# Ten stages of two model blocks in one program: the borders of the last four stages taken by halves of the tokens

## The chip, the cores and the metric

The program runs on one core of a Trainium2 chip. Its time is the device time of one launch in microseconds; the number given is the median of the runs shown. The engines are TensorE (PE), VectorE (DVE), ScalarE (ACT), GpSimd (POOL) and SyncE (SP), which here only issues the DMAs. They work at the same time, and only semaphores order them against each other.

## What is computed

x is an array of 512 tokens by 1024 numbers. Two blocks are applied to it, one after the other, all in float32:

```python
def swiglu_ffn(x, g, w_in, w_out):
    h = rms_norm(x, g)
    gate, up = jnp.split(h @ w_in, 2, axis=-1)
    return (jax.nn.silu(gate) * up) @ w_out

# first block, layers 0 and 1
x = x + 0.5 * swiglu_ffn(x, ffn1_norm[l], ...)
x = x + retention_dilated_mixer(...)  if l == 0 else x + stick_breaking_mixer(...)
x = x + 0.5 * swiglu_ffn(x, ffn2_norm[l], ...)
# then rms_norm(x, final_norm); second block, layers 0 and 1
def hybrid_layer(x, mod, norm1, norm2, ...):
    shift1, scale1, gate1, shift2, scale2, gate2 = jnp.split(mod[:, None, :], 6, axis=-1)
    h = rms_norm_2(x, norm1) * (1.0 + scale1) + shift1
    proj = h @ w_in                      # u, q, k and v, gates
    mix = jnp.concatenate([y_pool, y_nsa], axis=-1) @ w_out
    x = x + gate1 * mix
    h2 = rms_norm_2(x, norm2) * (1.0 + scale2) + shift2
    ff = jnp.square(jax.nn.relu(h2 @ w_ff1)) @ w_ff2
    return x + gate2 * ff
```

rms_norm divides each token by the root of the mean of its squares, so nothing that a stage does with a token can start before all 1024 numbers of that token are there. It needs no other token. Each of the second block's layers is a mixer (sparse attention y_nsa and a pooling y_pool) and a squared-relu feed-forward.

## The kernel before

There are ten stages: F1_0, HYB, F2_0, F1_1, STICK, F2_1 (first block), then NSA_0, REL_0, NSA_1, REL_1 (second block; NSA is a mixer, REL a feed-forward). The change is about the four borders F2_1 to NSA_0, NSA_0 to REL_0, REL_0 to NSA_1 and NSA_1 to REL_1.

**Layout.** x stands in SBUF as s_x, 128 partitions (features) by 8 tiles d by 512 tokens. A product is computed from split numbers: a float32 is a high part and a low part that PE multiplies at full rate, and one step k of a product is three matmuls of 512 columns (tokens): high input by high weight, low input by high weight, high input by low weight (`product`, L807). h is s_hh and s_hl, the middle activation s_a0h/s_a0l or s_a1h/s_a1l, the weights s_wh and s_wl.

**Weights** come in units of up to 1024 columns through a ring of four (RING): SP issues the DMA into s_raw, ACT copies s_raw to s_wh (L1355) and DVE subtracts to get s_wl (L1756). A ("load", u) in a plan is the place at which ACT and DVE convert unit u, three units ahead of PE (AHEAD). Each adds about 1 us to what stands behind it in ACT's and DVE's queues.

**Order.** Nothing is scheduled by a program. For each stage a function (`plan_ffn` L131, `plan_nsa` L345, `plan_rel` L440) writes one list of steps by hand, and every engine walks it and does its own part of each step, waiting on semaphores for the others. What an engine does is thus in the order of the list, and a step that waits holds all behind it on that engine.

**End of a stage.** Output tile d (one unit of weights, 8, 6 or, in the last part of NSA, 2 steps k) is a product into a PSUM bank; ("add") is DVE's scalar_tensor_tensor of 512 tokens from PSUM onto x (L1773); ("tile") is ACT's square of that tile and POOL's running sum over tiles 0 to 5 in s_ssum. For NSA_0 there is a second set of squares and sums with the gains of final_norm. The last tile's add and its squares are done in two halves of 256 tokens. The last part of NSA ("late", L423 to 437) has eight units of 256 columns.

**Head of a stage.** ("mean"): PE multiplies the squares of tiles 6 and 7 and s_ssum with ones (`norm_halves`, L1087: 12 records of 256 columns, 24 for NSA_0), ACT makes the roots from it (L1410), for NSA_0 after two small DVE steps (L2041). ("scale", d): DVE makes s_x times s_rstd (TENSOR_TENSOR, for NSA_0 scalar_tensor_tensor), then times and plus s_mod (TENSOR_SCALAR); ACT makes s_hh from the first of the two, DVE s_hl as the second less s_hh. ("first", four): PE runs the first four units together (`four`, L1297): for each k the high products of all four, the low-weight ones, the low-input ones, as soon as s_hh and s_hl of tile k are there.

The functions that the change touches:

Of the kernel before, what the change touches and what calls it, by code (L numbers as in the profile page):

```python
# [2840 lines left out]
```

## Time and profile before

| | |
|---|---|
| three runs | 3094.01, 3096.35, 3094.82 us; median 3094.82 |
| the profiled execution, first to last instruction | 3093.8 us |
| mean granted clock of PE in it | 0.997 of full speed |
| busy: PE, DVE, ACT, POOL | 3056.1, 1673.5, 1109.1, 680.3 us |
| matmul records of PE | 14530 |

The span is the profiled execution's own time from its first to its last instruction. The medians are of other executions, and lie within 1.0 us of that span. In a timeline "[3.66 <-ACT s_hh L76]" says that the engine was idle for 3.66 us before this row, and that ACT's write of s_hh ended the wait. A matmul's record is longer than the distance to the next one, since they are pipelined. All names of lines are those of small helpers (L70 is every matmul, L79 every tensor_tensor), so rows are told apart by the names of their tiles.

### The profile page before, as it was taken

Reading aid. Unit: us, or ns where it says so; the run is one execution under the profiler, and the core shown is the slowest. Engines: PE = TensorE matmul, PEld = TensorE weight load, DVE = VectorE, ACT = ScalarE, POOL = GpSimd, SP = SyncE. Lnnn points to the kernel's source line nnn. Section 1 sums busy time; section 2 is a strip of 40 time slices with the busy share of each in tenths; the row PEclk is TensorE's granted clock in tenths of the full one; section 3 lists DMA queues with packets and bytes.
Section 4 is the critical chain, followed back from the end, with each engine's and each line's share of the span. In section 5 each row is a group of like instructions: output and inputs, shape, how many; then the busy total and the mean of one; then the engine's idle time right before and its main releaser. Section 6 shows DMA issues by size and latency. Waiting matters only on the chain.

```text
span 3093.8 us, 36733 instructions
## 1 busy us (share of the span) xinstructions
PE 3056.1 (99%) x14530; PEld 2474.3 (80%) x14530; DVE 1673.5 (54%) x2491; ACT 1109.1 (36%) x1757; POOL 680.3 (22%) x525
## 2 busy tenths in 40 slices
PE   9999999999999999999999999999999999999999
PEld 7888887788888888887788888776788877778887
DVE  6454557554555445536864555677533356763332
ACT  4222344332223332244443222456422333643331
POOL 2101134111011110054211101356211123722110
PEclk9999999999999999999999999999999999999999
DMA  5343422243443334432043444301333331033332
GB/s 190 116 153 126 134 85 72 85 140 116 153 132 126 127 119 153 129 108 62 31 136 119 131 138 134 109 31 53 105 96 96 97 105 62 17 108 102 96 95 75
DMA packets 115802, 329.70 MB, mean 107 GB/s; under 512 B 13616, under 2 KB 19120, under 8 KB 115248
## 3 DMA queue, kind: packets, MB, share of 16 engines
q1 hardware_dynamic: 115632, 327.36, 33.1%
q8 instruction: 116, 1.90, 0.2%
q14 instruction: 54, 0.44, 0.0%
HBM read 325.21 MB, written 2.10 MB: 106 GB/s over the span
## 4 chain that ended last, share of the span: by engine, by line
PE 92%; DVE 4%; ACT 2%; POOL 1%; issue 1%; DMA 0%; DVEq 0%; SPq 0%; ACTq 0%; POOLq 0%
PE ps L70 90%; PE ps L73 1%; ACT s_tmp L76 1%; POOL s_tmp L87 1%; DVE s_tmp L79 1%; DVE s_wl L79 1%; DVE s_tmp L99 0%; ACT s_wh L76 0%; DVE s_small L93 0%; ACT s_hh L76 0%; DVE s_x L82 0%; DVE s_tmpr L79 0%; POOL s_tmp L79 0%; DVE s_hl L79 0%; ACT s_tmpr L76 0%
## 5 line engine op out<-in xcount | busy, mean ns | idle before, releaser
L76 ACT ACTIVATE s_wh<-s_raw 128x1024 fp32r<-128x1024 f32 (+3 forms) x560 | 541.8, 970 | 1109.3 <-PE ps L70 1107.2
L70 PE MATMUL ps<-s_hh,s_wh 128*128 128x512 f32 x2304 | 894.6, 393 | 18.8 <-ACT s_hh L76 11.9
L79 DVE TENSOR_TENSOR s_wl<-s_raw,s_wh 128x1024 fp32r<-128x1024 f32 (+3 forms) x529 | 607.8, 1150 | 532.6 <-ACT s_wh L76 532.3
L70 PE MATMUL ps<-s_hh,s_wl 128*128 128x512 f32 x2304 | 887.7, 390 | 0.2
L70 PE MATMUL ps<-s_hl,s_wh 128*128 128x512 f32 x2304 | 886.9, 390 | 0.3 <-DVE s_hl L79 0.3
L79 POOL TENSOR_TENSOR s_tmp<-s_tmp 128x512 f32<-128x512 f32 (+2 forms) x228 | 315.8, 1389 | 1616.5 <-ACT s_tmp L76 1453.3
L70 PEld LDWEIGHTS ps<-s_hh,s_wh 128*128 128x128 f32 x2304 | 433.3, 188 | 116.0 <-issue 17.1
L70 PEld LDWEIGHTS ps<-s_hh,s_wl 128*128 128x128 f32 x2304 | 433.6, 188 | 93.0 <-DVE s_wl L79 2.9
L70 PEld LDWEIGHTS ps<-s_hl,s_wh 128*128 128x128 f32 x2304 | 433.7, 188 | 92.2 <-issue 2.2
L70 PE MATMUL ps<-s_a0h,s_wh 128*128 128x512 f32 x960 | 377.3, 393 | 0.0
L70 PE MATMUL ps<-s_a0h,s_wl 128*128 128x512 f32 x960 | 373.8, 389 | 0.0
L70 PE MATMUL ps<-s_a0l,s_wh 128*128 128x512 f32 x960 | 373.7, 389 | 0.0
L70 PEld LDWEIGHTS ps<-s_a0h,s_wh 128*128 128x128 f32 x960 | 180.2, 188 | 38.6 <-issue 1.5
L70 PEld LDWEIGHTS ps<-s_a0h,s_wl 128*128 128x128 f32 x960 | 180.2, 188 | 37.8
L70 PEld LDWEIGHTS ps<-s_a0l,s_wh 128*128 128x128 f32 x960 | 180.3, 188 | 37.1 <-DVE s_a0l L79 0.3
L70 PE MATMUL ps<-s_a1h,s_wh 128*128 128x512 f32 x512 | 199.2, 389 | 0.0
L70 PE MATMUL ps<-s_a1l,s_wh 128*128 128x512 f32 x512 | 199.2, 389 | 0.0
L70 PE MATMUL ps<-s_a1h,s_wl 128*128 128x512 f32 x512 | 199.2, 389 | 0.0
L82 DVE SCALAR_TENSOR_TENSOR s_x<-ps,s_mod,s_x 128x512 f32<-128x512 f32 (+1 forms) x116 | 83.8, 729 | 196.5 <-PE ps L70 196.4
L79 DVE TENSOR_TENSOR s_a0l<-s_tmp,s_a0h 128x512 fp32r<-128x512 f32 x88 | 61.0, 693 | 170.9 <-ACT s_a0h L76 170.9
L82 DVE SCALAR_TENSOR_TENSOR s_x<-ps,s_x 128x512 f32<-128x512 f32 x129 | 88.2, 684 | 119.4 <-PE ps L70 119.4
L76 ACT ACTIVATE s_tmp<-ps 128x512 f32<-128x512 f32 (+6 forms) x258 | 132.9, 549 | 52.0 <-DVE s_tmp L79 20.2
(141 smaller groups left out, 2995.7 us busy)
## 6 DMA issues: line engine op xcount, KB each, us to landing
s_raw<-in_ff_dram SPq DMA_DIRECT2D x128, 512.0 KB, 3.6
s_tmp<-in_w_mod_dram SPq DMA_DIRECT2D x192, 256.0 KB, 3.5
s_raw<-in_f1i_dram SPq DMA_DIRECT2D x88, 512.0 KB, 3.6
s_raw<-in_f2i_dram SPq DMA_DIRECT2D x88, 512.0 KB, 3.6
s_raw<-in_f1o_dram SPq DMA_DIRECT2D x32, 512.0 KB, 3.5
s_raw<-in_f2o_dram SPq DMA_DIRECT2D x32, 512.0 KB, 3.4
s_raw<-in_hyb_dram SPq DMA_DIRECT2D x28, 512.0 KB, 3.5
s_raw<-in_nsa_dram SPq DMA_DIRECT2D x28, 512.0 KB, 3.6
```

The lines of the kernel that those rows point to most:

```text
L70: return self.eng.matmul(o, w, m, **kw) if self.eng is not None else Blank()
L73: return self.eng.transpose(*a) if self.eng is not None else Blank()
L76: return self.eng.activation(o, a, f, **kw) if self.eng is not None else Blank()
L79: return self.eng.tensor_tensor(o, a, b, f) if self.eng is not None else Blank()
L82: return self.eng.scalar_tensor_tensor(o, a, s, b, f, g) if self.eng is not None else Blank()
L87: return self.eng.tensor_scalar(o, a, s, t, f) if g is None else self.eng.tensor_scalar(o, a, s, t, f, g)
```

## The change

At the four borders the last output tiles are computed by halves of the tokens: of F2_1 tiles 5, 6 and 7, of REL_0 tiles 6 and 7, of both NSA the last part of all eight tiles. First comes tokens 0 to 255 of all these tiles, then 256 to 511 of all. Adds, squares and running sums of these tiles are by halves too.

The sum over tiles is one for each half (`sum_half` on PE; `norm_half` on ACT and DVE). That of tokens 0 to 255 stands before the end of the stage, among the last products ("next sum", "next mean"), and so do the first two tiles of the next stage's h for these tokens (`two_tiles`).

The next stage's first two units run by halves (`four`): for tokens 0 to 255 all eight high steps (four matmuls of 256 columns each), with the sum of tokens 256 to 511 behind the third, then all eight low-input steps (two matmuls each); then the same for 256 to 511. Units 3 and 4 run whole behind them, one after the other. The conversion of unit 3 stands between ACT's and DVE's scale steps and DVE's low steps of the second half, that of unit 4 behind the low steps (`head`).

s_hh and s_hl are made otherwise: DVE writes z = x times modulation times root (one scalar_tensor_tensor of 256 tokens), ACT adds the shift (s_hh), DVE makes s_hl from z, the shift and s_hh in one more. For that the gains of final_norm are multiplied into the modulation of NSA_0. The last part of NSA takes its weights as two units of 1024 columns, and uses four PSUM banks in turn (LATE_BANKS).

```diff
+HALVED = {F2_1: (5, 6, 7), NSA_0: tuple(range(KT)), REL_0: (6, 7), NSA_1: tuple(range(KT))}
+SUM_BANKS = {NSA_0: (6, 7), REL_0: (6, 7), NSA_1: (0, 1), REL_1: (6, 7)}
+LATE_BANKS = (4, 5, 2, 3)
+def two_tiles():
+    return [("next z", 0, 0), ("next h", 0, 0), ("next z", 1, 0), ("next h", 1, 0)]
+def head(four):
+    steps = []
+    for d in range(2, KT):
+        steps += [("z", d, 0), ("h", d, 0)]
+        if d == 4:
+            steps.append(("mean", 1))
+    steps += [("l", d, 0) for d in range(KT)]
+    for d in range(KT):
+        steps += [("z", d, 1), ("h", d, 1)]
+    return steps + [("load", four[2])] + [("l", d, 1) for d in range(KT)] + [("load", four[3])]
...
+                      ("half", 3, 6, u6, 1), ("add half", 3, 7, 0), ("tile half", 7, 0), ("next sum", 0),
+                      ("half", 3, 7, u7, 1), ("add half", 3, 6, 1), ("tile half", 6, 1), ("next mean", 0)] + two_tiles()
+                     + [("add half", 3, 7, 1), ("tile half", 7, 1)])
...
-    late = []
-    for d in range(KT):
-        u = stream.add(wo[d, :, 6 * 128:8 * 128], 256)
-        steps.append(("out", d, 6, 2, u))
...
+    late = [stream.add(wo[d:d + 4, :, 6 * 128:8 * 128].rearrange("d p c -> p d c"), 1024) for d in (0, 4)]
+    for n in range(2):
+        for d in range(KT):
+            steps.append(("half", 6, d, late[d // 4], n))
+            if d:
+                steps += [("add half", 6, d - 1, n), ("tile half", d - 1, n)]
+            if n == 0 and d == 1:
+                steps.append(("load", late[0] + AHEAD))
+            if n == 1 and d == 2:
+                steps.append(("next sum", 0))
+            if n == 1 and d == 3:
+                steps.append(("next mean", 0))
+            if n == 1 and d == 6:
+                steps += two_tiles()
+        steps += [("add half", 6, KT - 1, n), ("tile half", KT - 1, n)]
...
-            steps.extend([("mean",), ("scale", 0), ("load", four[3])] + [("scale", d) for d in range(1, KT)] + [("first", four)])
+            steps.extend(head(four) + [("first", four)])
...
+            def sum_half(s, n):
+                b, c = SUM_BANKS[s][n], HALVES[n]
...
+                for total, sig, slot, up, o, whole in sums:
+                    pe.wait_ge(*whole[sum_key(s, KT - 3, n)])
+                    pe.matmul(ps[:, b, o], ones[:, :], total[:, c], start=True, stop=False)
+                    for d in (KT - 2, KT - 1):
+                        pe.wait_ge(*sig[s, d, n])
+                        m = pe.matmul(ps[:, b, o], ones[:, :], S(slot(d))[:, c], start=False, stop=d == KT - 1)
+                    m.then_inc(*up.up((s, n)))
...
             def four(s, units_):
-                for k in range(KT - 2):
...
+                for n, c in enumerate(HALVES):
+                    for k in range(KT):
+                        cols = slice(k * 128, (k + 1) * 128)
+                        pe.wait_ge(*h_hi[h_key(s, k, n)])
+                        for u in units_[0:2]:
+                            pe.wait_ge(*w_hi[u])
+                            pe.matmul(ps[:, bank_of[u], c], wh[:, u % RING, cols], hh[:, k, c], start=k == 0, stop=False)
+                        for u in units_[0:2]:
+                            pe.wait_ge(*lo_of(u))
+                            pe.matmul(ps[:, bank_of[u], c], wl[:, u % RING, cols], hh[:, k, c], start=False, stop=False)
+                        if n == 0 and k == 2:
+                            sum_half(s, 1)
+                    for k in range(KT):
+                        cols = slice(k * 128, (k + 1) * 128)
+                        pe.wait_ge(*h_lo[h_key(s, k, n)])
+                        for u in units_[0:2]:
+                            m = pe.matmul(ps[:, bank_of[u], c], wh[:, u % RING, cols], hl[:, k, c], start=False, stop=k == KT - 1)
...
+            def scale(s, d, n):
...
+                if n:
+                    dve.wait_ge(*h_lo[s, d, "half"])
+                dve.scalar_tensor_tensor(scaled(d), x[:, d, c], mod[:, l, 3 * half + 1, d:d + 1], rstd[:, c], ALU.mult,
+                                         ALU.mult).then_inc(*h_scaled.up((s, d, n)))
...
+            def scale_lo(s, d, n):
...
+                dve.scalar_tensor_tensor(hl[:, d, c], scaled(d), mod[:, l, 3 * half, d:d + 1], f32(hh[:, d, c]),
+                                         ALU.add, ALU.subtract).then_inc(*h_lo.up(h_key(s, d, n)))
```

DVE's queue at the end of NSA_0, before: s_a0l is the last low part of the activation, s_wl a weight unit's low part, s_x the add of an output tile (signals: act_w_hi is ACT's conversion, pe_unit the end of a product).

```order
L79 TENSOR_TENSOR s_a0l<-ps,s_a0h 128x512 [waits act_a_hi]
L79 TENSOR_TENSOR s_wl<-s_raw,s_wh 128x256 [waits act_w_hi]
L82 SCALAR_TENSOR_TENSOR s_x<-ps,s_mod,s_x 128x512 [waits pe_unit]
L79 TENSOR_TENSOR s_wl<-s_raw,s_wh 128x256 [waits act_w_hi]
L82 SCALAR_TENSOR_TENSOR s_x<-ps,s_mod,s_x 128x512 [waits pe_unit]
L79 TENSOR_TENSOR s_wl<-s_raw,s_wh 128x256 [waits act_w_hi]
L82 SCALAR_TENSOR_TENSOR s_x<-ps,s_mod,s_x 128x512 [waits pe_unit]
L79 TENSOR_TENSOR s_wl<-s_raw,s_wh 128x256 [waits act_w_hi]
```

The same place now (pe_half is the end of a half product):

```order
L79 TENSOR_TENSOR s_a0l<-ps,s_a0h 128x512 [waits act_a_hi]
L79 TENSOR_TENSOR s_wl<-s_raw,s_wh 128x1024 [waits act_w_hi]
L82 SCALAR_TENSOR_TENSOR s_x<-ps,s_mod,s_x 128x512 [waits pe_unit]
L79 TENSOR_TENSOR s_wl<-s_raw,s_wh 128x1024 [waits act_w_hi]
L82 SCALAR_TENSOR_TENSOR s_x<-ps,s_mod,s_x 128x512 [waits pe_unit]
L82 SCALAR_TENSOR_TENSOR s_x<-ps,s_mod,s_x 128x256 [waits pe_half]
L79 TENSOR_TENSOR s_wl<-s_raw,s_wh 128x1024 [waits act_w_hi]
L82 SCALAR_TENSOR_TENSOR s_x<-ps,s_mod,s_x 128x256 [waits pe_half] x10
```

Three conversions of whole units stand where there was one of 256 columns for each add, and the last of them stands between the first and the second half add.

DVE's queue at the head of REL_0, before, from the first low step on (s_tmp is the scaled x):

```order
L79 TENSOR_TENSOR s_hl<-s_tmp,s_hh 128x512 [waits act_h_hi,dve_h_fine]
L79 TENSOR_TENSOR s_wl<-s_raw,s_wh 128x1024 [waits act_w_hi]
L79 TENSOR_TENSOR s_tmp<-s_x,s_rstd 128x512
L87 TENSOR_SCALAR s_tmp<-s_tmp,s_mod 128x512 [waits dve_h_scaled]
L79 TENSOR_TENSOR s_hl<-s_tmp,s_hh 128x512 [waits act_h_hi,dve_h_fine]
L79 TENSOR_TENSOR s_tmp<-s_x,s_rstd 128x512
L87 TENSOR_SCALAR s_tmp<-s_tmp,s_mod 128x512 [waits dve_h_scaled]
L79 TENSOR_TENSOR s_hl<-s_tmp,s_hh 128x512 [waits act_h_hi,dve_h_fine]
```

Now, from the scale steps of tokens 0 to 255 on:

```order
L82 SCALAR_TENSOR_TENSOR s_tmp<-s_x,s_mod,s_rstd 128x256 x6
L82 SCALAR_TENSOR_TENSOR s_hl<-s_tmp,s_mod,s_hh 128x256 [waits act_h_hi,dve_h_scaled] x8
L82 SCALAR_TENSOR_TENSOR s_tmp<-s_x,s_mod,s_rstd 128x256 [waits dve_h_lo,act_root2]
L82 SCALAR_TENSOR_TENSOR s_tmp<-s_x,s_mod,s_rstd 128x256 [waits dve_h_lo] x7
L79 TENSOR_TENSOR s_wl<-s_raw,s_wh 128x1024 [waits act_w_hi]
L82 SCALAR_TENSOR_TENSOR s_hl<-s_tmp,s_mod,s_hh 128x256 [waits act_h_hi,dve_h_scaled] x8
L79 TENSOR_TENSOR s_wl<-s_raw,s_wh 128x1024 [waits act_w_hi]
```

What went tile by tile now goes by phases of eight: scale steps, low steps, scale steps of the second half, the conversion of unit 3, low steps, the conversion of unit 4.

PE's queue at the head of REL_0, before:

```order
L70 MATMUL ps<-s_hh,s_wh 128x512 [waits act_h_hi,act_w_hi,dve_x_add]
L70 MATMUL ps<-s_hh,s_wh 128x512 [waits act_w_hi] x3
L70 MATMUL ps<-s_hh,s_wl 128x512 [waits dve_w_lo] x4
L70 MATMUL ps<-s_hl,s_wh 128x512 [waits dve_h_lo]
L70 MATMUL ps<-s_hl,s_wh 128x512 x3
L70 MATMUL ps<-s_hh,s_wh 128x512 [waits act_h_hi]
L70 MATMUL ps<-s_hh,s_wh 128x512 x3
L70 MATMUL ps<-s_hh,s_wl 128x512 x4
```

Now (s_ssum and s_tmp with s_ones are the sum of tokens 256 to 511):

```order
L70 MATMUL ps<-s_hh,s_wh 128x256 [waits act_h_hi]
L70 MATMUL ps<-s_hh,s_wh 128x256
L70 MATMUL ps<-s_hh,s_wl 128x256 x2
L70 MATMUL ps<-s_hh,s_wh 128x256 [waits act_h_hi]
L70 MATMUL ps<-s_hh,s_wh 128x256
L70 MATMUL ps<-s_hh,s_wl 128x256 x2
L70 MATMUL ps<-s_ssum,s_ones 128x256 [waits pool_ssum]
L70 MATMUL ps<-s_tmp,s_ones 128x256 [waits act_square] x2
L70 MATMUL ps<-s_hh,s_wh 128x256 [waits act_h_hi]
L70 MATMUL ps<-s_hh,s_wh 128x256
L70 MATMUL ps<-s_hh,s_wl 128x256 x2
```

Each step waits for one s_hh of 256 tokens and holds four matmuls of 256 columns where it held twelve of 512 with a wait for s_hl among them; the second sum stands between two steps.

## Rows read from the trace of the kernel before

**Rows 1.** The page's busy line: engine busy us (share of span) xinstructions.
```profile
PE 3056.1 (99%) x14530; PEld 2474.3 (80%) x14530; DVE 1673.5 (54%) x2491; ACT 1109.1 (36%) x1757; POOL 680.3 (22%) x525
```

**Rows 2.** PE's timeline: start, us, operation, count, idle before and releaser.
```profile
1955.64 2.04 PE L70 MATMUL ps<-s_hh,s_wh 128*128 128x512 f32 x4 [3.66 <-ACT s_hh L76]
...
2170.83 0.70 PE L70 MATMUL ps<-s_hh,s_wh 128*128 128x512 f32 x2 [2.99 <-ACT s_hh L76]
...
2525.18 1.25 PE L70 MATMUL ps<-s_hh,s_wh 128*128 128x512 f32 x4 [2.30 <-ACT s_hh L76]
```

**Rows 3.** Windows: us; PE, PEld, DVE, ACT, POOL busy (x); PEclk, DMA, GB/s.
```profile
1954.60:1961.40 6.80, 5.75 (x14) 4.53 (x15) 5.49 (x7) 2.56 (x4) 4.54 (x6) 0.50 0.94 329
...
2163.90:2174.20 10.30, 6.42 (x27) 4.38 (x25) 7.92 (x14) 7.95 (x14) 1.48 (x2) 1.00 0.54 177
```

**Rows 4.** PE's timeline: first matmul after the fourth unit, NSA_0 and NSA_1.
```profile
1980.22 0.39 PE L70 MATMUL ps<-s_wh,s_hh 128*128 128x512 f32 x1
...
2548.83 0.39 PE L70 MATMUL ps<-s_wh,s_hh 128*128 128x512 f32 x1
```

**Rows 5.** The chain of waits: start, us, operation, count.
```profile
1440.89 2.18 PE ps L73 x20
...
2174.11 345.75 PE ps L70 x1524
```

**Rows 6.** DVE's timeline at the adds named in the text.
```profile
1934.60 0.69 DVE L82 SCALAR_TENSOR_TENSOR s_x<-ps,s_x 128x512 f32<-128x512 f32 x1 [2.18 <-PE ps L70]
...
2153.29 0.75 DVE L82 SCALAR_TENSOR_TENSOR s_x<-ps,s_mod,s_x 128x512 f32<-128x512 f32 x1 [0.28 <-PE ps L70]
...
2509.01 0.75 DVE L82 SCALAR_TENSOR_TENSOR s_x<-ps,s_mod,s_x 128x512 f32<-128x512 f32 x1 [3.06 <-PE ps L70]
...
2519.89 0.88 DVE L82 SCALAR_TENSOR_TENSOR s_x<-ps,s_mod,s_x 128x256 f32<-128x256 f32 x2 [3.06 <-PE ps L70]
```

**Rows 7.** PE's timeline, the sum before NSA_0.
```profile
1946.64 2.32 PE L70 MATMUL ps<-s_tmp,s_ones 128*128 128x256 f32 x10
```

**Rows 8.** PE by form: count, busy us, mean ns, idle before and releaser.
```profile
L70 PE MATMUL ps<-s_tmpr 64*128 64x256 f32 x192 | 19.4, 306 | 2.7 <-DVE s_tmp L79 2.7
...
L70 PE MATMUL ps<-s_tmp,s_ones 128*128 128x256 f32 x40 | 10.7, 387 | 1.9 <-ACT s_tmp L76 1.9
```

**Rows 9.** PE's timeline, windows ending after two and three of one row's pairs.
```profile
2130.63 0.45 PE L70 MATMUL ps<-s_tmpr 64*128 64x256 f32 x4
...
2130.63 0.57 PE L70 MATMUL ps<-s_tmpr 64*128 64x256 f32 x6
```

**Rows 10.** ACT by form, 2164 to 2192, head of REL_0.
```profile
L76 ACT ACTIVATE s_wh<-s_raw 128x1024 fp32r<-128x1024 f32 x4 | 4.1, 1047 | 1.9 <-PE ps L70 1.9
...
L76 ACT ACTIVATE s_hh<-s_tmp,s_mod 128x256 fp32r<-128x256 f32 x2 | 1.1, 592 | 0.3 <-DVE s_tmp L79 0.3
...
L76 ACT ACTIVATE s_tmp<-ps,s_eps 128x256 f32<-128x256 f32 x2 | 0.9, 456 | 0.0
...
L76 ACT ACTIVATE s_rstd<-s_tmp 128x256 f32<-128x256 f32 x2 | 0.8, 416 | 0.1
...
L76 ACT ACTIVATE s_tmp<-s_x 128x256 f32<-128x256 f32 x2 | 0.7, 401 | 0.0
```

**Rows 11.** ACT's timeline, the first hh of REL_0.
```profile
2169.31 1.09 ACT L76 ACTIVATE s_hh<-s_tmp,s_mod 128x256 fp32r<-128x256 f32 x2 [0.26 <-DVE s_tmp L79]
```

**Rows 12.** DVE by form, 2168 to 2192, low parts of weight units.
```profile
L79 DVE TENSOR_TENSOR s_wl<-s_raw,s_wh 128x1024 fp32r<-128x1024 f32 x3 | 3.7, 1223 | 2.4 <-ACT s_wh L76 2.4
```

**Rows 13.** DVE by form, 1955 to 1976, with POOL at work and after.
```profile
L82 DVE SCALAR_TENSOR_TENSOR s_tmp<-s_x,s_gains,s_rstd 128x512 f32<-128x512 f32 x7 | 6.1, 870 | 0.0
...
L82 DVE SCALAR_TENSOR_TENSOR s_x<-s_x,s_gains,s_ssum 128x512 f32<-128x512 f32 x2 | 1.4, 747 | 0.0
```

**Rows 14.** DVE's timeline, the last a0l of NSA_0.
```profile
2150.98 0.69 DVE L79 TENSOR_TENSOR s_a0l<-ps,s_a0h 128x512 fp32r<-128x512 f32 x1 [3.20 <-ACT s_a0h L76]
```

**Rows 15.** POOL's timeline, two running-sum steps before REL_0.
```profile
2157.50 2.75 POOL L79 TENSOR_TENSOR s_ssum<-s_ssum,s_tmp 128x512 f32<-128x512 f32 x2 [0.73 <-ACT s_tmp L76]
```

More of the change, by code:

```diff
@@ L368, in plan_nsa @@
     four = [add_unit() for _ in range(4)]
-    steps += [("mean",), ("scale", 0), ("load", four[3])] + [("scale", d) for d in range(1, KT)] + [("x scale", d) for d in range(4)] + [("first", four)]
+    steps += head(four) + [("x scale", d) for d in range(4)] + [("first", four)]
     steps += [("load", four[3] + 1), ("copies", 0), ("load", four[3] + 2), ("copies", 1)] + [("x scale", d) for d in range(4, KT)] + [("u evac", 0), ("load", four[3] + 3)]
@@ L722, in last_add, with half_done @@
             p = {F1_0: 2, HYB: 1, F2_0: 2, F1_1: 2, STICK: 1, F2_1: 2, NSA_0: 6, REL_0: 3, NSA_1: 6}[s - 1]
-            return (s - 1, p, d) if half or finish_halves(s, d) == WHOLE else (s - 1, p, d, "half")
-        unit_at, bank_of = {}, {}
+            return (s - 1, p, d) if half or not halved(s, d) else (s - 1, p, d, "half")
+        unit_at, bank_of, half_bank = {}, {}, {}
+        def half_done(s, d, n):
+            u = unit_at[s, "half", d]
+            return unit[u] if n and (s not in (NSA_0, NSA_1) or d % 4 == 3) else half_up[s, d, n]
         def look_up():
@@ L905, in ffn @@
                         free[b] = [(x_add, (s, p, d))]
+                    elif kind == "half":
+                        half(s, *step[1:])
+                    elif kind == "next sum":
+                        sum_half(s + 1, 0)
                     elif kind == "modsum":
@@ L1113, in nsa @@
                     kind = step[0]
[L1114 to L1115 removed]
+                    if kind == "half":
+                        half(s, *step[1:])
+                    elif kind == "next sum":
+                        sum_half(s + 1, 0)
                     elif kind == "first":
@@ L1316, in rel @@
+                m.then_inc(*unit.up(u))
+                u, b = units_[3], bank_of[units_[3]]
+                claim(b)
+                product(b, u, h_of(s), range(KT), True, True).then_inc(*unit.up(u))
             def rel(s):
@@ L2418, in ffn @@
                         tile(s + 1, step[1])
+                    elif kind == "tile half":
+                        sum_tile(s + 1, step[1], step[2], HALVES[step[2]])
             def hyb(s):
@@ L2437, in hyb @@
                         tile(s + 1, step[1])
+                    elif kind == "tile half":
+                        sum_tile(s + 1, step[1], step[2], HALVES[step[2]])
             def stick(s):
@@ L2524, in nsa @@
                         tile(s + 1, step[1])
+                    elif kind == "tile half":
+                        sum_tile(s + 1, step[1], step[2], HALVES[step[2]])
             def rel(s):
@@ L2535, in rel @@
                         tile(s + 1, step[1])
+                    elif kind == "tile half":
+                        sum_tile(s + 1, step[1], step[2], HALVES[step[2]])
             for d in range(KT):
```

343 lines of the change are left out of this document (186 added, 157 removed).

## The prediction

> **What bounds the kernel now.** I read the page's busy line first [rows 1]: TensorE (PE) is busy 99% of the span, so the change can win only what PE loses at the four borders before and between the sparse stages, and it pays for all that it adds on PE. In the timeline of PE I looked at the first matmul behind each wait [rows 2]: it idles 3.66 us before the first unit of NSA_0, 2.99 before that of REL_0, 2.30 before that of NSA_1; REL_1 repeats REL_0. The windows show the granted clock [rows 3]: after the 3.66 us of idling it is 0.50, the 1.2 GHz level, for a stretch of 6.80 us; after the 2.99 us it stays at 1.00.
>
> What a border costs as a whole comes from its two ends. A matmul is shown 0.39 us long [rows 4] at a pace of 345.75/1524 = 0.227 [rows 5], so an add on VectorE (DVE), which waits for the shown end, starts 0.2 us after the slot of the product's last matmul. Border F2_1 to NSA_0: the product of tile 4 ends at 1934.60 - 0.2 = 1934.4 [rows 6], the fourth unit of NSA_0 at 1980.22 [rows 4]: 45.8 us. A record of the sums takes (2.32 - 0.387)/9 = 0.215 [rows 7, 8]. Work: 54 + 96 matmuls (34.1) and 24 records (5.2), 39.3; lost: 6.5, of it 2.8 to the clock: at half the clock each of the 14 matmuls that start in that stretch takes 0.2 more. NSA_0 to REL_0: the last early product ends at 2153.29 - 0.2 = 2153.1, the twelfth matmul of the head at 2174.11, 84 more take 19.1: 40.1 us for 48 + 96 matmuls and 12 records (35.3), lost 4.8. REL_0 to NSA_1: 2509.01 - 0.2 to 2548.83, 40.0 us for the same 35.3: lost 4.7. NSA_1 to REL_1 looks like the second. Lost at the four: 20.8 us. That is all there is to win.
>
> **The change part by part.** *Split products.* 54 matmuls of F2_1, 48 each of NSA_0, REL_0 and NSA_1, and 48 in each of four heads become two of 256 columns: 390 become 780. The sums keep their records. 512 columns at 2.4 GHz are 0.213 us, so 0.0135 of the 0.227 is a fixed part; 256 columns then cost 0.107 + 0.0135 = 0.120. Bounds: half of 0.227 is 0.1135 (nothing lost); above, of three pairs of 64-row matmuls with 256 columns two take 0.45 us and three 0.57 [rows 9]: the third adds 0.12, the second, with 0.306 for a lone one [rows 8], 0.144. That weights can be changed every 2.18/20 = 0.109 us is shown by the transposes [rows 5]. I take 0.120, the nearest row: 780 x 0.120 - 390 x 0.227 = 5.1 us (bounds 0 and 23.8).
>
> The trace has no full-height product of 256 columns. The Trainium skill ("TensorE: Matmul & The Clock Gate", Back-to-back issue gap) gives N/2.4 + 2.5 ns, 0.109 us at 256 and 0.216 at 512 columns. The trace disagrees at 512 with its 0.227. By the rule the split would cost 390 x 2.5 ns, 1.0 us (a rival below).
>
> *Prices off PE.* ACT: a half of hh 0.59, two in 1.09, so the next starts 0.50 later; a half square 0.40, the two root steps 0.46 and 0.42, a weight unit 1.05 [rows 10, 11]. DVE: low part of a weight unit 1.22 [rows 12]; a half scalar_tensor_tensor two in 0.88 [rows 6], which I read as 0.48 each with 0.40 between starts, an overlap of 0.08; an add of 512 columns 0.75, the next so 0.67 after its start. While POOL works beside it the 512 form takes 0.870 on average, else 0.747 [rows 13], and I put 0.50 for a half there. The new scale and low steps are such halves, 32 a border, 12.8 us at 0.40: just as much as what they hide behind, PE's first two units (96 x 0.120 = 11.5) and a sum (1.3), so they do not hide well.
>
> *End of NSA_0 (and of NSA_1).* A half product is 6 x 0.120 = 0.72 us. Its weights now come as two whole units, and three whole units (the second late one and REL_0's first two) are converted beside the first products. DVE: the last a0l ends at 2151.67 [rows 14]; ACT's unit, begun when its a0h is done, ends at 2151.9; low part to 2153.15, add 2153.8, low part 2154.95, add 2155.6, first half add 2156.05. ACT squares it (2156.45) and only then converts the fourth unit (2157.45); DVE's low part stands ahead of the second half add, which ends at 2159.1. PE has four banks for these products (LATE_BANKS); the sixth needs the bank of the second. It could start at 2153.1 + 4 x 0.72 + 0.1 + 0.72 = 2156.8: a new stall of 2.3 us, with 0.1 at the fifth. The sum of the first half waits for six steps of POOL, whole ones two in 2.75 us [rows 15], halves put at 0.7 to 0.9: 0 to 0.6, I take 0.3.
>
> *Head of the next stage.* PE's order: eight hh steps of 4 x 0.120 = 0.48 us each for tokens 0 to 255 with the second sum (1.3 us) behind the third, eight hl steps of 0.24, the same for 256 to 511, then two whole units (10.9 us). For REL_0:
> - hh 0 and 1 are made during the last products; 0.15 is lost.
> - hh 2 comes after the last half add (0.2 + 0.40), its scale step (0.47) and ACT (0.59): 1.7 us from the product's end against 0.96 of work: 0.6 to 0.75 lost.
> - On ACT the roots of the second half stand ahead of hh 5. After the sum: 0.2 + 0.46 + 0.42 + 0.59 with hand-overs is 1.7, against two steps of PE, 0.96: 0.7 lost.
> - DVE has the scale steps of the second half behind the last low step of the first. From there: eight scale steps 3.3, last hh 0.6, ACT's conversion of the third unit 1.05, its low part 1.22, and only then eight low steps 3.1: 9.3 us. PE's work from there is 2.0 + 3.84 + 1.92 = 7.8: 1.5 lost. The third unit is not needed before, but it stands in the queue ahead of the low steps, and everything behind them on PE waits.
>
> REL_0 so loses 2.4 + 0.3 + 0.15 + 0.6 + 0.7 + 1.5 = 5.7, against 4.8, and pays 96 x 0.0130 = 1.3 for its splits: +2.1; REL_1 the same. NSA_1 has no late weight stall (REL_0 halves only tiles 6 and 7): 0.75 + 0.7, and 2.5 behind the third unit, where POOL works beside it on the tables and half steps cost the 0.50 above: 4.0 against 4.7, splits 1.3: +0.5. NSA_0 has two more DVE steps and two more ACT steps in each root: 0.5 + 0.75 + 2.3, and 3.5 behind the third unit with POOL: 7.0 against 6.5, splits 1.4: +1.9. No single wait exceeds 2.4 us, so I count no fall of the clock there; the 2.8 us of before are in the 6.5.
>
> The larger late DMAs (512 KB in pieces of 1 KB) are issued over 5 us ahead; SP's tables move with the second sum; both cost nothing as long as that lead holds. Leading tiles in F2_1 and REL_0 feed sums in time.
>
> Sum: 2.1 + 2.1 + 0.5 + 1.9 = +6.6 us on a span of 3093.8. The runs' median, 3094.82, lies 1.0 above that span, so the time is 3094.8 + 6.6, about 3101.4 us. 6.2 us is 0.2%, about what a measurement of this kernel can tell from no change.
>
> **The rivals.**
> 1. *The borders really close* (faster). If a half step costs DVE and ACT half of a whole one (0.37 and 0.41) and the third unit's conversion fits between, the tail of the head vanishes (9 us of my 22.4) and the late stall shrinks from 2.4 to about 0.5 at two borders, the waits at the roots from 0.7 to 0.2 at four: 22.4 - 9 - 3.8 - 2 = 7.6 lost, 13.2 less than before, and 5.1 for the splits: -8, 3087 us. For it: the idle time before NSA_0's first unit is surely gone, hh 0 being made under the last product. Against: [rows 6, 10] show half steps at 60 to 70% of whole ones. It decides where the low steps of tokens 256 to 511 start before PE's hh steps end.
> 2. *A 256-column matmul is bound by its weight change* at 0.144 us [rows 8, 9]: 18.7 us more, of which about half fills waits counted above: +16, 3111 us. Against: the transposes' 0.109.
> 3. *The clock falls at the tails*, where PE is half busy for 3 us after a wait of 2: 2.8 us each by [rows 3], at two to four borders: 3107 to 3112. For it: the first line of [rows 3]; against: its second, with 2.99 us of idling and no fall.
> 4. *The fixed part is 2.5 ns*, the skill's gap above. As a mechanism of this kernel: 256 columns in half of 0.227, nothing lost by splitting (the low bound). PE then waits for DVE where it was late anyway, so only about half of the 5.1 comes back: 3099 us. The traced 0.227 speaks against a free split.
> 5. *The waits only change place* with no split cost showing: 3094 to 3096.
>
> **How the numbers follow.** Forecast 0.46 (3097 to 3107), rival 1 0.22, rival 2 0.10, rival 3 0.09, rival 4 0.08, rival 5 0.05. Of the forecast's 0.46, 0.23 lie above +6.2 us. Slower: 0.23 + 0.10 + 0.09 = 0.42; same: 0.23 + 0.08 + 0.05 = 0.36; faster: 0.22. The range 3087 to 3111 leaves out about half of rival 1 and of rival 2 and the end of rival 3.
>
> **What would show it.** In the profile after: 256-column products start 0.120 us apart (split); in NSA_0's end PE waits some 2 us once for DVE's s_x (late stall); in each head three waits on ACT's s_hh, at the third and sixth step, and one for DVE's s_hl or s_wl of about 1.5 us in REL and 2.5 to 3.5 in NSA; the granted clock stays 1.00 at 1954. I am wrong if the wait for s_hl is missing, or if the border from 2153.1 to the fourth unit's end is shorter than 40.1 us.

## The result and the profile after

| | before | changed |
|---|---|---|
| median of five runs | 3094.82 us (3093.3 to 3097.16) | 3110.21 us (3108.37 to 3110.98) |
| ratio, 95% interval | 1 | 1.0044 [1.0034, 1.0055] |
| profiled execution, span | 3093.8 us | 3108.6 us |

The changed kernel is 0.44% slower by the ratio (0.34 to 0.55%), 15.4 us by these medians and 14.8 by the spans. The forecast was 3101.4 us, with slower as the likeliest of three outcomes (0.42). The time lies 8.8 us above the forecast and 0.8 us inside the upper end of the range. The page's first lines, against [rows 1]:

```profile
span 3108.6 us, 37616 instructions
...
PE 3071.4 (99%) x14920; PEld 2503.2 (81%) x14920; DVE 1667.2 (54%) x2520; ACT 1112.6 (36%) x1792; POOL 679.8 (22%) x539
```

PE is busy 15.3 us longer, and its share is still 99%. This figure shows nothing of where: split matmuls overlap in the records, and matmuls at the lower clock count as busy. So I compared the starts of the same matmuls in the two timelines of PE, stage by stage. A border runs from the first matmul of the old stage's last output part to the first behind the new stage's fourth unit (for REL, to its first output product). The row "inside NSA_0" leaves out the stage's first 7.55 us, which are the same in all these kernels. The other kernels of the table are told of below.

| us | before | changed | x1 | x7 | x2 | x3 | x6 | x5 | x8 |
|---|---|---|---|---|---|---|---|---|---|
| F2_1 to NSA_0 | 66.65 | 69.09 | 69.09 | 70.62 | 66.35 | 68.48 | 66.34 | 63.49 | 62.94 |
| inside NSA_0 | 162.46 | 163.98 | 163.99 | 162.11 | 164.08 | 163.97 | 164.35 | 164.30 | 161.19 |
| NSA_0 to REL_0 | 108.34 | 112.46 | 110.09 | 109.19 | 110.80 | 112.22 | 107.34 | 106.60 | 106.49 |
| REL_0 to NSA_1 | 72.66 | 75.00 | 74.09 | 74.72 | 72.27 | 74.93 | 72.27 | 69.97 | 69.15 |
| inside NSA_1 | 171.93 | 171.48 | 171.30 | 171.83 | 169.86 | 171.78 | 172.04 | 169.85 | 171.78 |
| NSA_1 to REL_1 | 108.38 | 112.43 | 110.36 | 109.50 | 110.68 | 112.22 | 107.63 | 106.88 | 106.67 |

The insides of REL take 217.60 us in every kernel but x4. The changed kernel loses 2.4, 4.1, 2.3 and 4.1 us at the borders, 13.0 together where 6.6 was forecast, and 1.5 - 0.5 inside the two NSA stages; 0.9 more passes ahead of the first border, where nothing was changed. The ends of the new heads answer to [rows 4]:

```profile
1983.57 0.39 PE L70 MATMUL ps<-s_wh,s_hh 128*128 128x512 f32 x1
...
2560.16 0.39 PE L70 MATMUL ps<-s_wh,s_hh 128*128 128x512 f32 x1
```

PE's timeline shows the waits behind it (start, us, operation, count, idle before and releaser), against [rows 2]:

```profile
1959.21 0.53 PE L70 MATMUL ps<-s_hh,s_wh 128*128 128x256 f32 x1 [2.13 <-ACT s_hh L76]
...
2163.97 0.49 PE L70 MATMUL ps<-s_a0h,s_wh 128*128 128x256 f32 x1 [2.08 <-DVE s_x L82]
...
2177.08 0.39 PE L70 MATMUL ps<-s_hh,s_wh 128*128 128x256 f32 x1 [0.44 <-ACT s_hh L76]
...
2180.54 0.50 PE L70 MATMUL ps<-s_hh,s_wh 128*128 128x256 f32 x2 [0.47 <-ACT s_hh L76]
...
2188.27 3.27 PE L70 MATMUL ps<-s_hl,s_wh 128*128 128x256 f32 x16 [0.29 <-DVE s_hl L82]
...
2544.78 4.15 PE L70 MATMUL ps<-s_hl,s_wh 128*128 128x256 f32 x16 [1.60 <-DVE s_hl L82]
...
2740.51 0.39 PE L70 MATMUL ps<-s_a0h,s_wh 128*128 128x256 f32 x1 [2.07 <-DVE s_x L82]
```

Read the brackets in order. The 3.66 and 2.99 us before the first units are gone. In their place stand 2.13 us at NSA_0's sixth step of the first half, 2.08 for DVE's s_x in the last part of NSA_0, 0.44 and 0.47 at the third and sixth step of REL_0, 0.29 before its last low steps and 1.60 in NSA_1, then 2.07 at the end of NSA_1. The two rows with s_hl also show what a bracket hides: 16 matmuls of 256 columns take 3.27 and 4.15 us where 16 x 0.120 is 1.92, since DVE delivers a low step only every 0.40 us or more; in the second row the clock also fell on the way.

The windows of the changed kernel (columns as in [rows 3], the granted clock is the third number from the right):

```profile
1959.20:1962.80 3.60, 3.59 (x17) 3.59 (x18) 3.60 (x10) 1.73 (x5) 1.86 (x1) 0.53 0.90 343
2054.80:2062.00 7.20, 7.14 (x34) 5.04 (x34) 5.96 (x18) 2.48 (x5) 1.28 (x1) 0.53 0.03 4
2164.00:2167.60 3.60, 3.60 (x17) 3.60 (x18) 2.06 (x5) 2.25 (x6) 2.72 (x4) 0.53 0.52 146
2546.40:2550.00 3.60, 3.60 (x15) 3.34 (x15) 2.79 (x6) 1.18 (x2) 0.81 (x5) 0.53 0.12 43
2740.80:2744.40 3.60, 3.60 (x20) 3.60 (x20) 1.80 (x5) 2.17 (x6) 2.69 (x4) 0.53 0.40 148
```

A mean of 0.53 over a window of 3.6 us is 3.4 us at 0.50, the 1.2 GHz level, and over 7.2 us it is 6.8. The borders now have four such stretches, of 3.4 us each, where before there was one, of 6.8 us, at the first border. Three begin within 0.5 us of the end of a long wait above, the one at 2546.4 comes 1.6 us after the wait of NSA_1, while the low steps trickle in. The stretch inside NSA_0 (second row, 6.8 us) had half that length before:

```profile
2053.60:2057.20 3.60, 3.60 (x20) 2.39 (x20) 2.95 (x8) 1.27 (x3) 1.28 (x1) 0.53 0.00 0
```

### The profile page after: what moved, and what is told of

It is laid out like the page before. It is cut to its first block, busy times and chain, and to the rows that moved or that the text cites. A ratio compares the mean times of both kernels' runs of the same rounds, so it can differ in the third digit from the quotient of the medians.

```text
span 3108.6 us, 37616 instructions
## 1 busy us (share of the span) xinstructions
PE 3071.4 (99%) x14920; PEld 2503.2 (81%) x14920; DVE 1667.2 (54%) x2520; ACT 1112.6 (36%) x1792; POOL 679.8 (22%) x539
## 3 DMA queue, kind: packets, MB, share of 16 engines
q8 instruction: 119, 1.95, 0.3%
## 4 chain that ended last, share of the span: by engine, by line
PE 91%; DVE 4%; ACT 2%; POOL 1%; issue 1%; DMA 0%; SPq 0%; DVEq 0%; ACTq 0%; POOLq 0%
PE ps L70 90%; PE ps L73 1%; POOL s_tmp L87 1%; ACT s_tmp L76 1%; DVE s_tmp L79 1%; DVE s_wl L79 1%; DVE s_tmp L82 0%; ACT s_hh L76 0%; ACT s_wh L76 0%; DVE s_hl L82 0%; DVE s_tmp L99 0%; DVE s_small L93 0%; DVE s_x L82 0%; POOL s_tmp L79 0%; DMA s_raw<-in_f1i_dram 0%
## 5 line engine op out<-in xcount | busy, mean ns | idle before, releaser
L70 PE MATMUL ps<-s_hh,s_wh 128*128 128x512 f32 (+1 forms) x2368 | 908.1, 388 | 13.4 <-ACT s_wh L76 7.4
L70 PE MATMUL ps<-s_hl,s_wh 128*128 128x512 f32 (+1 forms) x2368 | 896.0, 386 | 3.3 <-DVE s_hl L82 2.8
L70 PE MATMUL ps<-s_hh,s_wl 128*128 128x512 f32 (+1 forms) x2368 | 894.7, 384 | 0.1
L70 PE MATMUL ps<-s_a0h,s_wh 128*128 128x512 f32 (+1 forms) x1010 | 388.6, 385 | 4.1 <-DVE s_x L82 4.1
L70 PE MATMUL ps<-s_a0h,s_wl 128*128 128x512 f32 (+1 forms) x1010 | 384.0, 380 | 0.0
L70 PE MATMUL ps<-s_a0l,s_wh 128*128 128x512 f32 (+1 forms) x1010 | 383.9, 380 | 0.0
L70 PE MATMUL ps<-s_a1h,s_wh 128*128 128x512 f32 (+1 forms) x528 | 202.2, 383 | 0.0
L70 PE MATMUL ps<-s_a1h,s_wl 128*128 128x512 f32 (+1 forms) x528 | 202.0, 383 | 0.0
L70 PE MATMUL ps<-s_a1l,s_wh 128*128 128x512 f32 (+1 forms) x528 | 202.0, 383 | 0.0
L82 DVE SCALAR_TENSOR_TENSOR s_x<-ps,s_x 128x512 f32<-128x512 f32 (+1 forms) x131 | 88.6, 676 | 119.8 <-PE ps L70 119.8
```

Source lines behind the costliest of these rows:

```text
L70: return self.eng.matmul(o, w, m, **kw) if self.eng is not None else Blank()
L82: return self.eng.scalar_tensor_tensor(o, a, s, b, f, g) if self.eng is not None else Blank()
```

## The experiments

Ratios are to the kernel before, timed on the same chip; their intervals are about 0.1%, 3 us, to either side. The changed kernel stood at 1.0044, about +13.6 us. Each edit is one to the changed kernel, but for x4.

### x1: the third conversion at the end of NSA, behind the sixth half product

```diff
-            if n == 0 and d == 1:
+            if n == 0 and d == 5:
                 steps.append(("load", late[0] + AHEAD))
```

> The changed kernel with one step moved: in the last part of both NSA stages the third conversion of a weight unit (the fourth unit of the next stage's ring, converted by ACT in 1.04 us and by DVE in 1.23) stands behind the sixth half product instead of behind the second. Theory (queue): PE's wait of 2.08 us at 2163.97 and 2.07 at 2740.51 comes from DVE doing this low part ahead of the second half add, and the spell of the lower clock around it (18 half matmuls 0.094 us longer, 1.7 us) comes from the wait; both go at both stages: about -7.5 us against the changed kernel (3110.2 to about 3102.7), and no wait for s_x over 0.5 us is left. Rival (banks): DVE and ACT cannot keep up with half products in four banks in any order; the wait moves to a later half product and keeps most of its size: 0 to -1.5 us.

Measured: 1.0024 [1.0015, 1.0034], 6 us better than the changed kernel. In the changed kernel DVE's queue at that place was:

```profile
2158.59 1.22 DVE L79 TENSOR_TENSOR s_wl<-s_raw,s_wh 128x1024 fp32r<-128x1024 f32 x1
2159.72 1.14 DVE L82 SCALAR_TENSOR_TENSOR s_x<-ps,s_mod,s_x 128x512 f32<-128x512 f32 x2
2162.30 1.23 DVE L79 TENSOR_TENSOR s_wl<-s_raw,s_wh 128x1024 fp32r<-128x1024 f32 x1 [1.43 <-ACT s_wh L76]
2163.44 1.65 DVE L82 SCALAR_TENSOR_TENSOR s_x<-ps,s_mod,s_x 128x256 f32<-128x256 f32 x4
```

The low part of 1.23 us, with 1.43 us of idling ahead of it for ACT, stands before the half adds of four finished products, as was forecast. In x1 it stands behind them, but still waits for ACT:

```profile
2163.53 1.42 DVE L79 TENSOR_TENSOR s_wl<-s_raw,s_wh 128x1024 fp32r<-128x1024 f32 x1 [1.70 <-ACT s_wh L76]
```

and PE waits less, later:

```profile
2165.40 0.39 PE L70 MATMUL ps<-s_a0h,s_wh 128*128 128x256 f32 x1 [1.23 <-DVE s_x L82]
...
2738.76 0.38 PE L70 MATMUL ps<-s_a0h,s_wh 128*128 128x256 f32 x1 [1.50 <-DVE s_x L82]
```

The queue's theory gives the direction, the banks' rival part of the size: of the waits of 2.08 and 2.07 us, 1.23 and 1.50 stayed. What went altogether is the fall of the clock at both places. The two borders take 2.4 and 2.1 us less. Another 0.9 us of the profile is at NSA_1's head, where the edit changed nothing and the clock did not fall this time.

### x7: the same conversion behind the sum

```diff
-            if n == 0 and d == 1:
-                steps.append(("load", late[0] + AHEAD))
             if n == 1 and d == 2:
-                steps.append(("next sum", 0))
+                steps += [("next sum", 0), ("load", late[0] + AHEAD)]
```

> The changed kernel with the third conversion at the end of both NSA stages moved once more: behind the sum of tokens 0 to 255 in the second pass, where DVE has nothing to add for the 1.3 us that the sum takes on PE. In x1_late_load it still held the half adds, since DVE idled 1.70 us for ACT's conversion and worked 1.42 us on it. Theory (queue): PE's wait for s_x is gone altogether, with the fall of the clock: -7.5 us against the changed kernel (its ratio to the kernel before 1.0044, so about 1.0020), or -1.5 us against x1. Rival (it only moves): the conversion now delays the roots of tokens 0 to 255 and the first s_hh, and PE waits there 1.5 us or more: no better than x1 (1.0024 or above).

Measured: 1.0023 [1.0014, 1.0031]. No wait for s_x of 0.2 us or more is left at NSA_0's end, and the border is 3.3 us shorter than in the changed kernel, the last one 2.9: together 6.2 of the 7.5 expected. On DVE:

```profile
2165.91 1.23 DVE L79 TENSOR_TENSOR s_wl<-s_raw,s_wh 128x1024 fp32r<-128x1024 f32 x1 [1.43 <-ACT s_wh L76]
2167.05 1.26 DVE L82 SCALAR_TENSOR_TENSOR s_x<-ps,s_mod,s_x 128x256 f32<-128x256 f32 x3
```

It idles 1.43 us for ACT, converts, and catches up with three adds, before PE runs out of banks. The ratio shows no gain over x1 all the same, and the two intervals can't tell them apart. In the profiles x7 is 1.8 us shorter than x1 at the two ends of NSA, and loses 1.5 at the first border, in which x7, x1 and the changed kernel have the same instructions. The wait at NSA_0's sixth step is the same 2.13 us in x7, but the clock did not fall behind it:

```profile
1958.00 0.50 PE L70 MATMUL ps<-s_hh,s_wh 128*128 128x256 f32 x2 [2.13 <-ACT s_hh L76]
...
1957.80:1961.40 3.60, 3.40 (x28) 3.41 (x29) 3.60 (x11) 1.72 (x5) 1.95 (x1) 1.00 0.85 294
```

It fell 9.5 us later, behind a wait of 1.79 us for s_hl, and for twice as long:

```profile
1967.20:1974.40 7.20, 7.08 (x23) 5.74 (x24) 7.20 (x12) 2.49 (x4) 3.94 (x10) 0.53 0.41 108
```

So two profiles of the same instructions can differ in where the clock falls and for how long. They also show what the fall at the sixth step costs: nothing. DVE's last low steps begin 53.2 us after the border's start in both. Without the fall PE only comes to them sooner and waits 1.95 us, start to start less the pace, where the changed kernel waits 0.43. What the timed runs did can't be seen, since they have no trace.

### x2: the conversion of unit 3 behind the low steps

```diff
-    return steps + [("load", four[2])] + [("l", d, 1) for d in range(KT)] + [("load", four[3])]
+    return steps + [("l", d, 1) for d in range(KT)] + [("load", four[2]), ("load", four[3])]
```

> The changed kernel with one step moved: in the head of all four stages the conversion of unit 3 stands behind the low steps of tokens 256 to 511 on DVE, not ahead of them. Theory (queue): DVE idles 1.55 us for ACT's conversion and works 1.23 us on it before the first low step, so these start 2.7 us earlier in REL; PE's wait for s_hl (0.29 us in REL, 1.60 in NSA_1) and the slow stretch of 16 half matmuls at 0.20 instead of 0.12 us go: -1.5 us in each REL, -2.5 in each NSA, together about -8 us. Unit 3's low weights are then ready about when PE has done its 16 high products (3.6 us). Rival (rate): the low steps cost DVE 0.40 us each and PE needs 0.24, so PE is held by DVE's rate wherever they start, and unit 3's low part comes late as well: between -1 and +2 us.

Measured: 1.0006 [0.9998, 1.0015], 11.8 us better than the changed kernel, the largest single cause. DVE at REL_0's head in the changed kernel:

```profile
2181.79 3.25 DVE L82 SCALAR_TENSOR_TENSOR s_tmp<-s_x,s_mod,s_rstd 128x256 f32<-128x256 f32 x8
2186.59 1.23 DVE L79 TENSOR_TENSOR s_wl<-s_raw,s_wh 128x1024 fp32r<-128x1024 f32 x1 [1.55 <-ACT s_wh L76]
2187.73 3.25 DVE L82 SCALAR_TENSOR_TENSOR s_hl<-s_tmp,s_mod,s_hh 128x256 fp32r<-128x256 f32 x8
```

and in x2:

```profile
2178.82 3.25 DVE L82 SCALAR_TENSOR_TENSOR s_tmp<-s_x,s_mod,s_rstd 128x256 f32<-128x256 f32 x8
2181.99 3.25 DVE L82 SCALAR_TENSOR_TENSOR s_hl<-s_tmp,s_mod,s_hh 128x256 fp32r<-128x256 f32 x8
2185.16 2.35 DVE L79 TENSOR_TENSOR s_wl<-s_raw,s_wh 128x1024 fp32r<-128x1024 f32 x2
```

Between the last scale step and the first low step stood 2.7 us (1.55 of idling and 1.23 of work, overlapping a little); now the low steps follow at once, and unit 3's low part comes in time. The wait for s_hl is gone in both REL stages and NSA_0, and 0.37 us long in NSA_1. The borders take 2.7, 1.7, 2.7 and 1.8 us less, 8.9 together, and the fall of the clock at 2546 is gone. Another 1.6 us of the profile is inside NSA_1, which the edit does not touch and where the clock was low for 3.4 us and not 6.8. DVE's rate, the rival, did not bind at three borders: eight steps at 0.40 us, begun 2.7 us earlier, are ahead of PE. In NSA_1, where POOL works at the same time, DVE takes 5.30 us for the eight, and PE's 16 low matmuls still take 1.6 us more than 16 x 0.120:

```profile
2536.25 5.30 DVE L82 SCALAR_TENSOR_TENSOR s_hl<-s_tmp,s_mod,s_hh 128x256 fp32r<-128x256 f32 x8
```

### x3: the second roots behind the last s_hh

```diff
-        if d == 4:
+        if d == 7:
             steps.append(("mean", 1))
```

> The changed kernel with one step moved: in the head of all four stages the roots of tokens 256 to 511 on ACT (for NSA_0 also two small DVE steps) stand behind the eighth s_hh of tokens 0 to 255, not behind the fifth. Theory (queue): ACT waits for PE's sum while s_hh 5 could be made; PE's wait at the sixth step (0.47 us in REL and NSA_1, 2.13 in NSA_0, there with 22 matmuls at the lower clock) goes: about -0.6 three times and -4 in NSA_0, -5.5 us together. Rival (given back): the scale steps of tokens 256 to 511 need this root, start later by what it is delayed, and the low steps at the end of the head come later by the same: about 0 us.

Measured: 1.0043 [1.0031, 1.0056], no change: the rival was right. ACT in the changed kernel at REL_0's head:

```profile
2179.16 0.48 ACT L76 ACTIVATE s_tmp<-ps,s_eps 128x256 f32<-128x256 f32 x1 [1.33 <-PE ps L70]
2179.67 0.42 ACT L76 ACTIVATE s_rstd<-s_tmp 128x256 f32<-128x256 f32 x1
2179.99 1.29 ACT L76 ACTIVATE s_hh<-s_tmp,s_mod 128x256 fp32r<-128x256 f32 x3
```

It idles 1.33 us for PE's sum with s_hh 5 to 7 behind it. In x3 that wait is gone at REL_0, and PE waits here instead:

```profile
1966.23 0.39 PE L70 MATMUL ps<-s_hl,s_wh 128*128 128x256 f32 x1 [1.96 <-DVE s_hl L82]
...
2186.39 0.39 PE L70 MATMUL ps<-s_hl,s_wh 128*128 128x256 f32 x1 [0.76 <-DVE s_hl L82]
```

At NSA_0 2.13 us at the sixth step became 1.96 before the low steps, with a fall of the clock behind that; at REL_0 0.29 became 0.76. The time was given back to the next wait down the chain, not in the way the rival had put it: the root was in time for the scale steps, but the conversion of unit 3 held the low steps where they were.

### x4: splitting alone, in the kernel before

```diff
-                        product(b, u, a_of(s, p), range(KT), True, True).then_inc(*unit.up(u))
+                        for c in HALVES:
+                            m = product(b, u, a_of(s, p), range(KT), True, True, cols=c)
+                        m.then_inc(*unit.up(u))
```

> The kernel before (whole borders) in which every output product of both REL stages (64 units, 1536 matmuls of 512 columns) is computed as two products of 256 columns, one after the other into the two halves of the same bank: 3072 matmuls. Nothing waits for a half. At 0.120 us for 256 columns, as in the changed kernel's trace, it costs 1536 x 0.013 = 20 us (3094.8 to about 3115); if splitting were free, 0; if the weight change bound it at 0.144 us, 94 us.

Measured: 1.0061 [1.0045, 1.0076], +18.9 us (13.9 to 23.5) against 20 expected. The same 20 us of an output part, first before and then x4:

```profile
2260.00:2280.00 20.00, 20.00 (x90) 16.57 (x89) 7.77 (x8) 4.20 (x5) 1.59 (x1) 1.00 0.34 98
```

```profile
2260.00:2280.00 20.00, 20.00 (x169) 20.00 (x168) 7.03 (x8) 3.82 (x4) 1.31 (x1) 1.00 0.29 99
```

90 matmul records of 512 columns become 169 of 256. A record counts while it overlaps the window, two at the edges, so the pace is 20/88 = 0.227 and 20/167 = 0.120. That is 0.013 us a split: neither free nor bound by the weights. The start-to-start times agree: inside REL_0, 576 splits add 7.7 us.

x4 shows one thing more. It leaves the border NSA_0 to REL_0 as it was in the kernel before, where the clock stayed at 1.00 behind 2.99 us of idling [rows 3]. Here it fell behind 2.82 us at the same matmul, and the border takes 109.15 us and not 108.34:

```profile
2169.09 1.89 PE L70 MATMUL ps<-s_hh,s_wh 128*128 128x512 f32 x4 [2.82 <-ACT s_hh L76]
...
2169.20:2172.80 3.60, 3.60 (x9) 2.80 (x10) 3.01 (x5) 1.40 (x2) 0.00 (x0) 0.53 0.60 184
```

### x6, x5 and x8: together

x6 is x7 and x2 together, x5 adds the edit of x3. x8 is x5 with three tiles of the next h made inside the old stage, in NSA two of them one output tile earlier:

```diff
-    return [("next z", 0, 0), ("next h", 0, 0), ("next z", 1, 0), ("next h", 1, 0)]
+    return [(what, d, 0) for d in range(3) for what in ("next z", "next h")]
...
-    for d in range(2, KT):
+    for d in range(3, KT):
...
-            if n == 1 and d == 6:
-                steps += two_tiles()
+            if n == 1 and d == 5:
+                steps += two_tiles()[0:4]
+            if n == 1 and d == 6:
+                steps += two_tiles()[4:6]
```

> x7_late_gap and x2_tail_load together. Theory (two separate waits on one queue): they add up, -7.5 and -11.8 us, together 19 us below the changed kernel, 5 to 6 us below the kernel before (ratio about 0.998). Rival (one chain): the head of the next stage is bound by DVE and ACT from the last half add on, so what the late part gains is waited for in the head; then it is as x2_tail_load, ratio 1.0006, or at most 2 us below it.

> x6_late_tail and the roots of tokens 256 to 511 behind the eighth s_hh, as in x3_mean_last. There it brought nothing (ratio 1.0043), the wait came back before the low steps. Theory (what was given back was given back to the conversion of unit 3 that stood there): with that out of the way the 0.63 us at three borders and the 2.29 at NSA_0 with its slow matmuls are kept, -4 us against x6. Rival (DVE's rate): the low steps bind the end of the head in any case, no difference to x6 within 1 us.

> x5_all, in which three tiles of the next stage's h for tokens 0 to 255 instead of two are made before the last half add, and in NSA the first two of them one output tile earlier. Theory: PE's three small waits at the start of each head (0.30, 0.24 and 0.60 us at 2175 to 2177 in the changed kernel, 0.48 and 0.43 before NSA_0) go for the most part: -0.8 us a border, -3 us against x5. Rival: the third tile delays the last half add, its square and so the second sum: within 1 us of x5.

| | ratio, 95% interval | median | span |
|---|---|---|---|
| x6 | 0.9987 [0.9978, 0.9996] | 3092.7 us | 3093.6 us |
| x5 | 0.9964 [0.9951, 0.9976] | 3086.1 us | 3083.1 us |
| x8 | 0.9956 [0.9942, 0.9970] | 3082.9 us | 3081.1 us |

The kernel before had a median of 3096.4 us beside them. The profiled execution of x6 was a long one, 3095.4 us. x6 is 17.6 us below the changed kernel: the two conversions are separate waits and add up. x5 is another 7 us below x6: the same edit that was worth nothing alone is worth more than the 4 us expected once the conversion is out of its way. The borders take 2.8, 0.7, 2.3 and 0.8 us less. In NSA_1 most of it is that DVE's eight low steps took 3.25 us there and no longer held PE. PE's wait at NSA_0's sixth step (2.13 us in the changed kernel) is:

```profile
1959.04 0.50 PE L70 MATMUL ps<-s_hh,s_wh 128*128 128x256 f32 x2 [0.43 <-ACT s_hh L76]
```

x8 is 3.3 us below x5 by the medians, with overlapping intervals; its borders are 0.55 + 0.11 + 0.82 + 0.21 = 1.7 us shorter in the table, where 3 was expected. What the third tile is worth is thus not shown by the times alone. Against the kernel before x8 is 13.6 us faster, with all the splits of the change in it. Its windows over the four borders:

```profile
1944.00:1983.00 39.00, 38.25 (x271) 34.10 (x271) 34.79 (x61) 23.41 (x45) 21.30 (x18) 1.00 0.41 126
2145.00:2190.00 45.00, 44.62 (x282) 40.11 (x282) 34.84 (x63) 27.69 (x53) 14.80 (x16) 1.00 0.31 100
2500.00:2545.00 45.00, 45.00 (x332) 41.31 (x332) 30.82 (x52) 22.88 (x41) 21.11 (x18) 1.00 0.42 143
2710.00:2755.00 45.00, 44.41 (x281) 39.97 (x281) 35.07 (x63) 27.70 (x53) 14.58 (x16) 1.00 0.33 100
```

The granted clock is 1.00 in all four, against 0.50 in the first row of [rows 3].

## Why the prediction was right, and by how little

The range of 3087 to 3111 us was wide enough for a gain as well as a loss, and the time lies 0.8 us inside its end. It lies outside the forecast's own 3097 to 3107 us and among the times of rivals 2 and 3, which together had a chance of 0.19. The direction and most terms were right by their mechanism; that the range held was partly luck.

**The splits** (+5.1 us, bounds 0 and 23.8): right. The pace is 0.120 us, here the starts of two neighbouring matmuls in the changed kernel,

```profile
1943.59 0.28 PE L70 MATMUL ps<-s_a0h,s_wh 128*128 128x256 f32 x1
1943.71 0.28 PE L70 MATMUL ps<-s_a0l,s_wh 128*128 128x256 f32 x1
```

and x4 measures 0.013 a split over 1536 of them. The Trainium skill's rule ("TensorE: Matmul & The Clock Gate", Back-to-back issue gap), which the page calls the gap of an isolated matmul, gives 0.109 for 256 columns. The trace disagrees by 0.011 a matmul, as at 512 columns; the gap that it would need is 13, not 2.5 ns. Rivals 2 and 4 are out.

**The late stall** (2.3 and 0.1 us at each NSA's end): right, with 2.08 us in the bracket and 2.24 from start to start less the pace, in the place and for the engine named. x1 and x7 show its cause, the low part ahead of the half adds.

**The head's small waits** (0.15, 0.6 to 0.75, 0.7, together 1.5): 0.30, 0.24, 0.60 and 0.63 at REL_0, start to start less the pace, together 1.8. NSA_0's 2.3 us at the roots is 2.29.

**The tail behind unit 3** (1.5 in REL, 2.5 in NSA_1, 3.5 in NSA_0): the cause is shown by x2. REL_0 lost 0.45 us at the wait and 1.2 in the slow low steps: right. NSA_1 lost 1.1 and 2.3 where the clock did not fall (x1), together 3.4 and 0.9 more than the forecast. NSA_0 lost 0.43 and 2.3 in the changed kernel, but only because the lower clock had delayed PE before; in x7, without that fall, it lost 1.95 and 2.6, of the latter 0.3 by the clock, so 0.8 more than the forecast. The mechanism was right, and both NSA terms were too small: DVE's eight low steps, put at 0.50 us each beside POOL, took 4.17 to 4.58 us in these profiles, 0.52 to 0.57 each.

**The clock**: the step that failed. "No single wait exceeds 2.4 us, so I count no fall of the clock there" took the 2.99 us of [rows 2] without a fall for a bound. It was no bound: in x4 the clock fell at that very place. In the changed kernel it fell after 2.13, 2.08, 1.60 and 2.07 us. The sign "the granted clock stays 1.00 at 1954" came true by its letter alone, since the fall there came at 1959.3. A half matmul at the lower level starts 0.213 us after the last, 0.093 more than at the upper. That makes 17 x 0.093 = 1.6 and 16 x 0.093 = 1.5 us at the two ends of NSA; at NSA_1's head it is 0.9, since x1, with the same instructions and no fall there, takes 74.09 us and not 75.00. At NSA_0's head 15 matmuls lost 1.4 us that PE would otherwise have waited for DVE, as x7 shows, so there it cost nothing. The forecast had no fall at any border. These 4.0 us are the largest part of the 6.4 by which the borders came out above it; the two NSA tails are 1.7, and the rest is of the size of the small waits. It was rival 3's mechanism, mostly at another place: that rival had the falls where PE is half busy in the tails, and three of the four came right behind the stalls. Its price of 2.8 us each was too high, since the stretches were half as long as that of [rows 3]. In the profiles the falls went when the waits did: in x7 both at the ends of NSA, in x2 the one at 2546, in x5 that at NSA_0's head.

**What is left over**: of the 14.8 us, 13.0 are at the borders. 1.5 more are a longer low stretch inside NSA_0, whose instructions did not change; 0.5 less passed in NSA_1, 0.9 more ahead of the borders. The insides of NSA in the table go by the low stretch that a profile happened to have there. NSA_0 takes 161.2 us without one (x8), 162.1 to 162.5 with 3.4 us of it (x7, before) and 164.0 to 164.4 with 6.8 (the others); NSA_1 takes 169.9 with 3.4 us (x2, x5) and 171.3 to 172.0 with 6.8. The changed kernel has 6.8 us in both, so nothing shows that this part of its span belongs to the change.

Rival 1, that the borders really close, was false for this order of steps and true for another: its gain of 8 us is passed by x5 (11) and x8 (14). My argument against it, that half steps cost 60 to 70% of whole ones, holds (0.40 us for DVE's, eight in 3.25) and was no reason: this rate is enough as soon as nothing else stands among the steps.

## What to carry to other kernels

Splitting a stage's border in halves makes many short steps on the helping engines, and one long step left among them (here a weight conversion of 1.0 + 1.2 us, first on one engine and then on the next) costs more than the splitting: move it to where the queue is idle or its result late in demand. Here 0.44% slower became 0.36% faster (x5) with all the splits still in place, by moving two conversions and the second sum's roots. An edit that gives nothing alone is to be tried again when the wait that took its gain is gone. And price a wait of 2 us on PE not by its length alone but with the matmuls at half the clock that may follow it, where PE is what the next step waits for. One profile without a fall is no proof that none comes.
